# Splitting the first block's branch outputs into an attention half and a convolution half, and leaving 28 convolution taps until after the attention

## The chip, the cores and the metric

The kernel runs on one core of a Trainium2 chip. The metric is the device time of one execution in microseconds (us), the median of several runs. A difference of about 0.3% is what a measurement of this kernel can tell from no change.

The core has five engines that this document speaks of by the profile's names: PE (TensorE, matrix products; PEld is its weight load), DVE (VectorE), ACT (ScalarE), POOL (GpSimd) and SP (SyncE, which here issues the weight transfers). Each runs its own list of instructions in order; they wait for each other by semaphores. SBUF is the on-chip memory, PSUM the eight banks into which PE accumulates.

## The reference, cut to what matters

Two transformer blocks on 512 tokens of width 1024, all in float32. The change touches the first block alone, between its attention and the product with `w_out`:

```python
y_attn = nsa_attention(q, ...) @ w_attn_br[l]
y_conv = conformer_conv(u_conv, conv_dw_w[l], conv_dw_b[l], conv_ln_g[l], conv_ln_b[l], w_conv_br[l])
g_a, g_b = jnp.split(jax.nn.sigmoid(g_merge), 2, axis=-1)
x = x + (g_a * y_attn + g_b * y_conv) @ w_out[l]
```

```python
def conformer_conv(u, dw_w, dw_b, ln_g, ln_b, w_proj):
    a, gate = jnp.split(u, 2, axis=-1)
    z = a * jax.nn.sigmoid(gate)
    z = causal_dwconv(z, dw_w) + dw_b        # 31 taps, 512 channels
    z = jax.nn.silu(layer_norm(z, ln_g, ln_b))
    return z @ w_proj
```

## The kernel before, in words

**Layout and weights.** Activations lie transposed: channels on the 128 partitions, 512 tokens along the row. Every large product is cut into *units*. A unit is 128x1024 weights: eight blocks of 128x128, each used in three float32r matmuls of 512 columns (high part by high part, high by low, low by high), 24 matmuls in all. SP loads a unit's raw weights into one of five slots as soon as PE has finished with the unit five places earlier (`unit_done`); POOL then splits them into `whi` (L1055, L1056) and `wlo = raw - whi` (L1059); PE waits for `w_split`. So POOL's work comes once per unit, at the pace at which PE finishes units. The table `UNITS` gives the order of the units, here ... `ga` 0 to 7, `gb` 0 to 7, `y` 0 to 7, `wout` 0 to 7.

**Attention loop.** 32 steps (4 head pairs, 2 branches, 4 query tiles). In each, PE does scores (L568), transposes (L578), a quarter of a `ga` unit (six matmuls, L461) and values (L590). Scores go into two PSUM banks, one per half, and PE may write the next step's scores only when DVE has read these (`n_max`, L1847). DVE does `n_max` and, between, the *taps*: the convolution of the second branch is 4 chunks of channels times 31 taps = 124 instructions `cacc = z*w + cacc` (L1721), each on 128x512 elements, two of its inputs in SBUF. 46 of them are done before the loop. In the loop `taps(1)` is called in each of the first 12 steps and the other 66 are spread over the last 20 (4 or 3 a step). The attention to compressed keys adds more DVE work in the first ten steps (L1886 to L1906).

**After the attention.** PE does `gb` 1 to 7. Between them it takes column sums for the layer norm of the convolution: `mu` sums (four of them, one for each channel chunk, L515) after `gb` 1, a broadcast of the mean (`spread`, L549) after `gb` 2, variance sums after `gb` 3 and 4, their broadcast after `gb` 5. DVE centers (L1917), computes the reciprocal root, scales (L1928), and with ACT does SiLU (L1935 with ACT L1316 and L1321) and splits the result in high and low parts (ACT L1325, DVE `low_z` L1940). Then come eight `y` units. Unit `y` i makes output chunk i: half 0 is `w_attn_br` (four blocks, 12 matmuls, into bank 2 or 3), half 1 is `w_conv_br` (bank 6 or 7). DVE merges per chunk: L1982 multiplies the attention part by its gate, L1986 the convolution part, L1989 adds; ACT makes the high part (L1328), DVE the low part (L1975). The eight `wout` units take those as input; the first of them waits chunk by chunk.

## Time and profile before

| | us |
|---|---|
| median of 3 runs | 1352.49 |
| lowest, highest | 1349.76, 1352.93 |
| the profiled execution | 1354.35 |
| its span | 1351.9 |

| engine | busy us | share of the span |
|---|---|---|
| PE | 1313.4 | 97% |
| PEld | 1034.9 | 77% |
| DVE | 824.1 | 61% |
| POOL | 647.6 | 48% |
| ACT | 442.4 | 33% |

Durations below are from the profiled execution, which is 1.9 us above the median; its span is the time from the first to the last record, and 2.5 us lie around it. PE's busy time is modelled at its ends: matmuls overlap, so one that is listed with 0.39 us is followed by the next after 0.23 us. The pace is to be read from starts.

### The profile page before, as it was taken

The numbers are of one execution on the slowest core, as the hardware profiler recorded it, in microseconds if no ns is written. First come the engines' busy times: TensorE is split into PE (matmuls) and PEld (weight loads), VectorE is DVE, ScalarE is ACT, GpSimd is POOL, SyncE is SP. The second block draws the span as 40 slices with busy tenths as digits, with TensorE's granted clock in tenths as the row PEclk, the third lists the DMA queues.
The fourth block names the chain that finished last, engine by engine and source line by source line (L and its number), as shares of the span: only waits on it lengthen the run. The fifth ranks groups of instructions, "written<-read, shape, count | busy, mean of one in ns | idle before, by whom it ended". The sixth has DMA issues, their size and how long they took to land. (4 is left out here: it accounts for less than half of the span.)

```text
span 1351.9 us, 19692 instructions
## 1 busy us (share of the span) xinstructions
PE 1313.4 (97%) x7254; PEld 1034.9 (77%) x7254; DVE 824.1 (61%) x1586; ACT 442.4 (33%) x948; POOL 647.6 (48%) x523
## 2 busy tenths in 40 slices
PE   7999999999999999999999999999999999899996
PEld 5898776688888888888888888876657888666675
DVE  4898689914554777777773546536765552156643
ACT  4201555523121211222110432256665231244521
POOL 5775222246676666666676365532000566523230
PEclk9999999999999999999999989999999999899998
DMA  4622110112253455555552124211000223211011
GB/s 180 241 67 78 32 43 22 47 62 80 94 174 123 156 197 199 195 187 190 195 176 94 60 90 155 78 48 32 1 1 1 94 69 95 76 48 32 32 48 62
DMA packets 37522, 130.24 MB, mean 96 GB/s; under 512 B 4544, under 2 KB 4800, under 8 KB 37184
## 3 DMA queue, kind: packets, MB, share of 16 engines
q1 hardware_dynamic: 26640, 93.11, 21.2%
q10 hardware_dynamic: 10800, 35.98, 7.2%
q8 instruction: 58, 0.95, 0.3%
q14 instruction: 24, 0.20, 0.1%
HBM read 126.98 MB, written 2.10 MB: 95 GB/s over the span
## 5 line engine op out<-in xcount | busy, mean ns | idle before, releaser
L1059 POOL TENSOR_TENSOR wlo<-raw,whi 128x1024 fp32r<-128x1024 f32 x171 | 419.2, 2451 | 14.3
L1055 POOL TENSOR_TENSOR whi<-raw,ones 128x2 fp32r<-128x2 f32 x171 | 48.8, 285 | 654.2 <-DMA raw<-in_w 654.0
L461 PE MATMUL bank<-ysplit,whi 128*128 128x512 f32 x984 | 313.3, 397 | 0.9 <-POOL wlo L1059 0.9
L461 PE MATMUL bank<-hhi,whi 128*128 128x512 f32 x536 | 219.0, 409 | 0.8 <-DVE arena L2179 0.4
L461 PEld LDWEIGHTS bank<-ysplit,whi 128*128 128x128 f32 x984 | 183.6, 189 | 37.3 <-POOL wlo L1059 1.3
L461 PE MATMUL bank<-hhi,wlo 128*128 128x512 f32 x536 | 210.7, 393 | 0.0
L461 PE MATMUL bank<-hlo,whi 128*128 128x512 f32 x536 | 210.2, 392 | 0.0
L461 PE MATMUL bank<-ysplit,wlo 128*128 128x512 f32 x496 | 194.2, 392 | 0.0
L1056 POOL TENSOR_SCALAR whi<-raw 128x1022 fp32r<-128x1022 f32 x171 | 186.0, 1088 | 0.0
L461 PEld LDWEIGHTS bank<-hhi,whi 128*128 128x128 f32 x536 | 101.4, 189 | 26.3 <-issue 7.3
L461 PEld LDWEIGHTS bank<-hhi,wlo 128*128 128x128 f32 x536 | 101.4, 189 | 22.3
L461 PEld LDWEIGHTS bank<-hlo,whi 128*128 128x128 f32 x536 | 101.8, 190 | 18.3
L461 PEld LDWEIGHTS bank<-ysplit,wlo 128*128 128x128 f32 x496 | 93.7, 189 | 20.1
L1721 DVE SCALAR_TENSOR_TENSOR arena<-first,arena 128x512 f32<-128x512 f32 x120 | 103.5, 912 | 0.2
L1346 ACT ACTIVATE arena<-bank,cols 128x512 f32<-128x512 f32 x44 | 34.4, 781 | 177.7 <-DVE bank L2041 177.7
L2203 DVE CUSTOM_DVE_ANT_0 arena<-bank,arena 128x512 f32<-128x512 f32 x64 | 44.2, 690 | 44.6 <-PE bank L864 26.6
L760 PE MATMUL bank<-hhi,whi 128*128 128x512 f32 x176 | 68.5, 389 | 0.0
L760 PE MATMUL bank<-hlo,whi 128*128 128x512 f32 x176 | 68.5, 389 | 0.0
L760 PE MATMUL bank<-hhi,wlo 128*128 128x512 f32 x176 | 68.5, 389 | 0.0
L2041 DVE TENSOR_TENSOR bank<-bank,arena 128x512 f32<-128x512 f32 x44 | 30.7, 699 | 50.4 <-PE bank L461 50.4
L1460 ACT ACTIVATE arena<-arena,nmax,stat 128x512 f32<-128x512 f32 x64 | 51.6, 808 | 12.8 <-DVE nmax L2207 10.2
L2025 DVE CUSTOM_DVE_ANT_0 arena<-bank,arena 128x512 f32<-128x512 f32 x80 | 51.7, 683 | 0.0
(315 smaller groups left out, 2105.5 us busy)
## 6 DMA issues: line engine op xcount, KB each, us to landing
raw<-in_w SPq DMA_DIRECT2D x171, 512.0 KB, 3.6
arena<-in_ada ACTq DMA_DIRECT2D x48, 512.0 KB, 4.3
xbuf<-in_xT ACTq DMA_DIRECT2D x12, 256.0 KB, 5.6
xbuf<-in_w ACTq DMA_DIRECT2D x1, 2048.0 KB, 11.3
first<-in_w ACTq DMA_DIRECT2D x1, 2048.0 KB, 8.3
out_t<-xbuf SPq DMA_DIRECT2D x8, 256.0 KB, 2.1
xbuf<-in_xT SPq DMA_DIRECT2D x4, 256.0 KB, 6.4
first<-in_uq ACTq DMA_DIRECT2D x1, 768.0 KB, 7.1
```

The source lines that it names most:

```text
L461: m = mm(b[:, :], w[:, s, k * P:(k + 1) * P], x, start=(k == 0 and part == 0), stop=(k == DC - 1 and part == 2))
L760: m = mm(b[:, :], w[:, u % WS, n * P:(n + 1) * P], x, start=(i == 0 and part == 0), stop=(i == FC - 1 and part == 2))
L1055: g.tensor_tensor(whi[:, s, 0:2], raw[:, s, 0:2], ones[:, :], ALU.mult)
L1056: g.tensor_scalar(whi[:, s, 2:D], raw[:, s, 2:D], 1.0, 1.0, ALU.mult, ALU.mult)\
L1059: g.tensor_tensor(wlo[:, s, :], raw[:, s, :], whi[:, s, :].bitcast(F32), ALU.subtract)\
L1346: A(ua[:, i % 4, :], bank.of(("up", i))[:, :], ACT.Identity, scale=col("ffw", order_up(i) * 3 + 2), bias=col("ffb", order_up(i)))\
L1460: A(abp[:, s % 3, half, :], abp[:, s % 3, half, :], ACT.Exp, bias=nmax[:, x:x + 1], scale=ab_scale(p, half, qt), accum_out=rsum[:, x:x + 1 ...
L1721: V.scalar_tensor_tensor(cacc[:, c, :], z[:, c, k:k + T], w, cacc[:, c, :], ALU.mult, ALU.add)\
L2025: V.tensor_tensor_reduce(ada[:, j % 2, at], bank.tiles[CACT[half]][:, :], ada[:, j % 2, at], 1.0, 0.0, ALU.mult, ALU.add, acc[:, j // (3 * ...
L2041: V.tensor_tensor(b[:, :], b[:, :], spread2, ALU.mult).then_inc(*dve_did.up(("un", i)))
L2203: link(V.tensor_tensor_reduce(abp[:, s % 3, half, :], bank.of(("S", "AB", s, half))[:, :], zero, 1.0, -3.0e38, ALU.add, ALU.max, nmax[:, x ...
```

## The change

1. The eight `y` units become four `ya` units and four `yc` units. A `ya` unit holds the attention weights of two output chunks, a `yc` unit the convolution weights of two. The bytes, the units and the matmuls are the same; the order is all of the attention's first. A new function `y_unit` does one; each half goes into the next of four banks (2, 3, 6, 7) and signals for itself.
2. The layer norm's work on PE moves back: `mu` sums from behind `gb` 1 to behind `gb` 5, their broadcast to behind `gb` 6, variance sums behind `gb` 7 and `ya` 0, their broadcast behind `ya` 1. ACT's squares and SiLU parts move with them.
3. `TAPS_LIGHT` goes, `TAPS_NSA = 50` comes: 50 taps are spread evenly over the 32 steps (1 or 2 a step), and the remaining 28 are done in one run when DVE has left the attention loop.
4. DVE multiplies the attention part by its gate in eight instructions `y_attn(0)` to `y_attn(7)`, placed between the layer norm's parts; the last loop then has, for each chunk, the convolution part's product, the sum and the low part.

```diff
@@ -49,7 +49,7 @@
     + [("q", i) for i in range(4)]
     + [("ga", i) for i in range(DC)]
     + [("gb", i) for i in range(DC)]
-    + [("y", i) for i in range(DC)]
+    + [("ya", i) for i in range(4)] + [("yc", i) for i in range(4)]
...
@@ -85,7 +85,8 @@
 PREP_Q = {12: 0, 13: 1, 16: 2, 17: 3, 20: 4, 21: 5, 24: 6, 25: 7}
 AB_FILL = [("ega", 3), ("egb", 0), ("egb", 1), ("egb", 2), ("egb", 3)]
 EOUT_FIRST = {32: ((0, 0, 3),), 33: ((0, 3, 6),), 34: ((1, 0, 7), (0, 6, 7)), 35: ((2, 0, 7),)}
-TAPS_LIGHT = 12
+TAPS_NSA = 50
+Y_BANKS = (2, 3, 6, 7)
 CMP_S, CMP_TURN, CMP_O, N_HIGH = (1, 3, 5, 7), (5, 7, 9, 11), (13, 15, 16, 17), (18, 20, 28, 36)
...
-LIN, SC, TR, OB = (0, 1), (2, 3), (4, 5), (6, 7)
+LIN, SC, TR = (0, 1), (2, 3), (4, 5)
...
@@ -710,34 +711,42 @@
                 if i in CMP_O:
                     cmp_values(CMP_O.index(i))
 
+            def y_unit(name, j):
+
+                u, c0 = UNIT[(name, j)], 4 if name == "yc" else 0
+                pe.wait_ge(w_split.sem, u + 1)
+                for half in range(2):
+                    if j == 0 and half == 0:
+                        for c in range(4):
+                            pe.wait_ge(*dve_did.at(("y", c0 + c)))
+                    b = bank.take(pe, Y_BANKS, (name, 2 * j + half))
+                    for k in range(4):
+                        kk = 4 * half + k
+                        for part, (w, x) in enumerate(((whi, yhi(c0 + k)), (whi, ylo(c0 + k)), (wlo, yhi(c0 + k)))):
+                            m = mm(b[:, :], w[:, u % WS, kk * P:(kk + 1) * P], x,
+                                   start=(k == 0 and part == 0), stop=(k == 3 and part == 2))
+                    if half == 0:
+                        m.then_inc(*pe_did.up((name, 2 * j)))
+                m.then_inc(*unit_done.up(u))
+
             for i in range(1, DC):
                 unit("gb", i)
-                if i == 1:
+                if i == 5:
                     stats("mu", CC, src=cacc, ready=lambda c: dve_did.at(("conv", c)))
-                if i == 2:
+                if i == 6:
                     spread("mu", 2)
-                if i == 3:
+                if i == 7:
                     sums("var", 0, CC)
                     sums("var", 1, CC)
-                if i == 4:
+            for j in range(4):
+                y_unit("ya", j)
+                if j == 0:
                     sums("var", 2, CC)
                     sums("var", 3, CC)
-                if i == 5:
+                if j == 1:
                     spread("var", 4)
-            for i in range(DC):
-                u = UNIT[("y", i)]
-                pe.wait_ge(w_split.sem, u + 1)
-                for half, pool in ((0, SC), (1, OB)):
-                    if i == 0:
-                        for c in range(4):
-                            pe.wait_ge(*dve_did.at(("y", 4 * half + c)))
-                    b = bank.take(pe, pool, ("y", i, half))
-                    for k in range(4):
-                        kk = 4 * half + k
-                        for part, (w, x) in enumerate(((whi, yhi(kk)), (whi, ylo(kk)), (wlo, yhi(kk)))):
-                            m = mm(b[:, :], w[:, u % WS, kk * P:(kk + 1) * P], x,
-                                   start=(k == 0 and part == 0), stop=(k == 3 and part == 2))
-                m.then_inc(*unit_done.up(u))
+            for j in range(4):
+                y_unit("yc", j)
 
             for i in range(DC):
                 unit("wout", i, first=(lambda k: dve_did.at(("m", k))) if i == 0 else None)
@@ -1307,22 +1316,20 @@
 
             for i in range(DC):
                 gb_evac(i)
-                if i == 2 or i == 3:
-                    for c in (2 * i - 4, 2 * i - 3):
+                if i >= 6:
+                    for c in (2 * i - 12, 2 * i - 11):
                         square("var", c, cacc[:, c, :], dve_did.at(("zc", c)))
-                if i == 5:
-                    for c in range(CC):
-                        act.wait_ge(*dve_did.at(("zn", c)))
-                        A(cacc[:, c, :], cacc[:, c, :], ACT.Identity, scale=col("lng", c), bias=col("lnb", c))\
-                            .then_inc(*act_did.up(("zu", c)))
-                        if c >= 2:
-                            act.wait_ge(*dve_did.at(("zs", c - 2)))
-                        act.wait_ge(*act_did.at(("zu", c)))
-                        A(hs[:, c % 2, :], cacc[:, c, :], ACT.Tanh, scale=0.5).then_inc(*act_did.up(("zt", c)))
-                if i == 6:
-                    for c in range(CC):
-                        act.wait_ge(*dve_did.at(("zs", c)))
-                        A(yhi(4 + c), cacc[:, c, :], ACT.Copy, scale=0.5).then_inc(*act_did.up(("zhi", c)))
+            for c in range(CC):
+                act.wait_ge(*dve_did.at(("zn", c)))
+                A(cacc[:, c, :], cacc[:, c, :], ACT.Identity, scale=col("lng", c), bias=col("lnb", c))\
+                    .then_inc(*act_did.up(("zu", c)))
+                if c >= 2:
+                    act.wait_ge(*dve_did.at(("zs", c - 2)))
+                act.wait_ge(*act_did.at(("zu", c)))
+                A(hs[:, c % 2, :], cacc[:, c, :], ACT.Tanh, scale=0.5).then_inc(*act_did.up(("zt", c)))
+            for c in range(CC):
+                act.wait_ge(*dve_did.at(("zs", c)))
+                A(yhi(4 + c), cacc[:, c, :], ACT.Copy, scale=0.5).then_inc(*act_did.up(("zhi", c)))
             for i in range(DC):
                 act.wait_ge(*dve_did.at(("mg", i)))
                 A(hhi[:, i, :], merged[:, i, :], ACT.Copy, scale=0.5).then_inc(*act_did.up(("mhi", i)))
@@ -1958,17 +1965,38 @@
                 if i - 1 in N_HIGH:
                     o_low(N_HIGH.index(i - 1))
                 if i < n:
-                    taps(1 if i < TAPS_LIGHT else -(-len(steps) // (n - i)))
+                    taps((i + 1) * TAPS_NSA // n - i * TAPS_NSA // n)
+            taps(len(steps))
+
+            def y_attn(i):
+
+                if i % 2:
+                    dve.wait_ge(*unit_done.at(UNIT[("ya", i // 2)]))
+                else:
+                    dve.wait_ge(*pe_did.at(("ya", i)))
+                if i == 0:
+                    dve.wait_ge(*act_did.at(("ga", DC - 1)))
+                V.scalar_tensor_tensor(merged[:, i, :], merged[:, i, :], 1.0, bank.of(("ya", i))[:, :],
+                                       ALU.add, ALU.mult).then_inc(*dve_did.up(("ya", i)))
+                bank.freed(("ya", i), dve_did, ("ya", i))
+
             neg_mean()
             for c in range(CC):
                 center(c)
+            y_attn(0)
             var_rstd()
+            y_attn(1)
+            y_attn(2)
             for c in range(CC):
                 scale_z(c)
+            y_attn(3)
             for c in range(CC):
                 silu_z(c)
+            y_attn(4)
             for c in range(CC):
                 low_z(c)
+            for i in range(5, DC):
+                y_attn(i)
 
             def merged_low(i):
                 dve.wait_ge(*act_did.at(("mhi", i)))
@@ -1976,16 +2004,17 @@
                                        ALU.mult, ALU.subtract).then_inc(*dve_did.up(("m", i)))
 
             for i in range(DC):
-                dve.wait_ge(*unit_done.at(UNIT[("y", i)]))
-                if i == 0:
-                    dve.wait_ge(*act_did.at(("ga", DC - 1)))
-                link(V.scalar_tensor_tensor(merged[:, i, :], merged[:, i, :], 1.0, bank.of(("y", i, 0))[:, :],
+                if i % 2:
+                    dve.wait_ge(*unit_done.at(UNIT[("yc", i // 2)]))
+                else:
+                    dve.wait_ge(*pe_did.at(("yc", i)))
+                dve.wait_ge(*act_did.at(("gb", i)))
+                if i:
+                    dve.wait_ge(*dve_did.at(("mg", i - 1)))
+                link(V.scalar_tensor_tensor(ytmp, gbt[:, i, :], 1.0, bank.of(("yc", i))[:, :],
                                             ALU.add, ALU.mult))
-                bank.freed(("y", i, 0), dve_did, ("link", dve_did.n - 1))
-                dve.wait_ge(*act_did.at(("gb", i)))
-                link(V.scalar_tensor_tensor(ytmp, gbt[:, i, :], 1.0, bank.of(("y", i, 1))[:, :],
-                                            ALU.add, ALU.mult))
-                bank.freed(("y", i, 1), dve_did, ("link", dve_did.n - 1))
+                bank.freed(("yc", i), dve_did, ("link", dve_did.n - 1))
+                dve.wait_ge(*dve_did.at(("ya", i)))
                 V.tensor_tensor(merged[:, i, :], merged[:, i, :], ytmp, ALU.add)\
                     .then_inc(*dve_did.up(("mg", i)))
@@ -2403,7 +2432,8 @@
         "k": lambda i: col(w_in, (at[3], at[5], at[1], at[2])[i]),
         "ga": lambda i: col(w_in, at[9] + i * P),
         "gb": lambda i: col(w_in, at[9] + D + i * P),
-        "y": lambda i: np.concatenate([col(a["w_attn_br"][0][n_rows], i * P), col(a["w_conv_br"][0], i * P)]),
+        "ya": lambda i: np.concatenate([col(a["w_attn_br"][0][n_rows], j * P) for j in (2 * i, 2 * i + 1)]),
+        "yc": lambda i: np.concatenate([col(a["w_conv_br"][0], j * P) for j in (2 * i, 2 * i + 1)]),
         "wout": lambda i: col(a["w_out"][0], i * P),
         "up": lambda i: col(up, order_up(i) * P),
```

The order of the instructions, as the two programs have it. Names are tiles: `arena` holds among much else the convolution's sums `cacc`, `first` its input `z`, `xbuf` the merged branch outputs, `ysplit` the high and low parts that PE multiplies, `bank` a PSUM bank.

DVE at the end of the attention, before (L1865 to L1877 finish the last head pair, L1911 is the mean, L1917 the centering):

```order
307 L1865 TENSOR_TENSOR hs<-bank,arena 128x512
308 L1869 TENSOR_TENSOR first<-first,hs 128x512
309 L1873 TENSOR_TENSOR first<-first 128x512
310 L1877 TENSOR_TENSOR ysplit<-first,ysplit 128x512
311 L1911 TENSOR_SCALAR stat<-bank 128x4
312 L1917 TENSOR_TENSOR arena<-arena,bank 128x512 x4
313 L1599 TENSOR_SCALAR bank<-bank 128x4
```

and in the changed kernel (its line numbers are 7 higher here; L1728 is the tap, L1979 is `y_attn`):

```order
307 L1872 TENSOR_TENSOR hs<-bank,arena 128x512
308 L1876 TENSOR_TENSOR first<-first,hs 128x512
309 L1880 TENSOR_TENSOR first<-first 128x512
310 L1884 TENSOR_TENSOR ysplit<-first,ysplit 128x512
311 L1728 SCALAR_TENSOR_TENSOR arena<-first,arena 128x512 x28
312 L1918 TENSOR_SCALAR stat<-bank 128x4
313 L1924 TENSOR_TENSOR arena<-arena,bank 128x512 x4
314 L1979 SCALAR_TENSOR_TENSOR xbuf<-xbuf,bank 128x512
315 L1606 TENSOR_SCALAR bank<-bank 128x4
```

28 taps have come between the attention's last low part and the mean, and the first `y_attn` stands between the centering and the variance.

DVE from the scaling by the reciprocal root to the merge, before:

```order
325 L1928 TENSOR_TENSOR arena<-arena,bank 128x512 x4
326 L1935 SCALAR_TENSOR_TENSOR arena<-hs,arena 128x512 x4
327 L1940 SCALAR_TENSOR_TENSOR ysplit<-arena,ysplit 128x512 x4
328 L1982 SCALAR_TENSOR_TENSOR xbuf<-xbuf,bank 128x512
329 L1986 SCALAR_TENSOR_TENSOR arena<-arena,bank 128x512
330 L1989 TENSOR_TENSOR xbuf<-xbuf,arena 128x512
```

and in the changed kernel:

```order
327 L1979 SCALAR_TENSOR_TENSOR xbuf<-xbuf,bank 128x512 x2
328 L1935 TENSOR_TENSOR arena<-arena,bank 128x512 x4
329 L1979 SCALAR_TENSOR_TENSOR xbuf<-xbuf,bank 128x512
330 L1942 SCALAR_TENSOR_TENSOR arena<-hs,arena 128x512 x4
331 L1979 SCALAR_TENSOR_TENSOR xbuf<-xbuf,bank 128x512
332 L1947 SCALAR_TENSOR_TENSOR ysplit<-arena,ysplit 128x512 x4
333 L1979 SCALAR_TENSOR_TENSOR xbuf<-xbuf,bank 128x512 x3
334 L2014 SCALAR_TENSOR_TENSOR arena<-arena,bank 128x512
335 L2018 TENSOR_TENSOR xbuf<-xbuf,arena 128x512
```

The attention's products stand in two places within the layer norm's chain and three behind it; the merge of a chunk is one product shorter.

PE at the `mu` sums, with its waits, before (the rows around are the last block of `gb` 1 and the first of `gb` 2):

```order
948 L461 MATMUL bank<-hhi,wlo 128x512
949 L515 MATMUL bank<-ones,arena 128x1 [waits ptc,dve_did]
950 L515 MATMUL bank<-ones,arena 128x1 x3
951 L515 MATMUL bank<-ones,arena 128x1 [waits dve_did]
952 L515 MATMUL bank<-ones,arena 128x1 x3
```

and in the changed kernel (around are `gb` 5 and `gb` 6):

```order
1044 L462 MATMUL bank<-hhi,wlo 128x512
1045 L516 MATMUL bank<-ones,arena 128x1 [waits ptc,dve_did]
1046 L516 MATMUL bank<-ones,arena 128x1 x3
1047 L516 MATMUL bank<-ones,arena 128x1 [waits dve_did]
1048 L516 MATMUL bank<-ones,arena 128x1 x3
```

The sums stand 96 matmuls, four units, further back; the waits for DVE's last taps are the same.

## Rows read from the trace of the kernel before

**Rows 1.** The page: busy us (share of the span) and instructions

```profile
PE 1313.4 (97%) x7254; PEld 1034.9 (77%) x7254; DVE 824.1 (61%) x1586; ACT 442.4 (33%) x948; POOL 647.6 (48%) x523
```

**Rows 2.** Waits of PEld, 185 to 275 us: line, released by, us, times, longest

```profile
PEld bank L568 <- DVE nmax L1847: 5.9, 4, 2.3
PEld bank L568 <- DVE arena L1721: 0.8, 1, 0.8
```

**Rows 3.** PE timeline: start, us, engine line op, tiles, count [idle before, releaser]

```profile
260.01 0.79 PE L568 MATMUL bank<-split_r 64*128 64x384 f32 x6 [2.08 <-DVE nmax L1847]
```

**Rows 4.** DVE: source view of L1721 (ns min/median/max), then timeline of taps

```profile
L1721 DVE SCALAR_TENSOR_TENSOR arena<-first,arena x120: 734/742/2876, 56.5 to 268.6; 128x512 f32<-128x512 f32 x120
...
90.46 18.41 DVE L1721 SCALAR_TENSOR_TENSOR arena<-first,arena 128x512 f32<-128x512 f32 x24
...
223.07 4.20 DVE L1721 SCALAR_TENSOR_TENSOR arena<-first,arena 128x512 f32<-128x512 f32 x3
```

**Rows 5.** POOL timeline: the split after those taps, and the one at 223 us

```profile
109.57 0.20 POOL L1055 TENSOR_TENSOR whi<-raw,ones 128x2 fp32r<-128x2 f32 x1 [15.82 <-DMA raw<-in_w]
...
223.21 2.85 POOL L1059 TENSOR_TENSOR wlo<-raw,whi 128x1024 fp32r<-128x1024 f32 x1
```

**Rows 6.** Steps 2 and 3 of the attention: DVE's timeline, then PE's

```profile
144.22 0.55 DVE L1847 CUSTOM_DVE_ANT_0 arena<-bank,arena 128x384 f32<-128x384 f32 x1
...
144.92 0.98 PE L568 MATMUL bank<-split_r 64*128 64x512 f32 x6
```

**Rows 7.** PE timeline: first matmul of gb 1, and the mu sums behind it

```profile
278.86 0.39 PE L461 MATMUL bank<-hhi,whi 128*128 128x512 f32 x1
...
284.30 3.63 PE L515 MATMUL bank<-ones,arena 128*128 128x1 f32 x32
```

**Rows 8.** DVE timeline: the last instruction of the attention

```profile
280.96 0.69 DVE L1877 TENSOR_TENSOR ysplit<-first,ysplit 128x512 fp32r<-128x512 f32 x1 [0.70 <-ACT ysplit L1282]
```

**Rows 9.** POOL timeline behind the attention: the low splits

```profile
284.14 2.35 POOL L1059 TENSOR_TENSOR wlo<-raw,whi 128x1024 fp32r<-128x1024 f32 x1
...
289.56 2.38 POOL L1059 TENSOR_TENSOR wlo<-raw,whi 128x1024 fp32r<-128x1024 f32 x1
```

**Rows 10.** Windows (busy, granted clock, DMA) at two places, a wait of PE

```profile
288.00:290.00 2.00, 2.00 (x8) 1.60 (x8) 0.12 (x1) 0.00 (x0) 1.65 (x3) 0.78 0.00 0
290.00:292.00 2.00, 2.00 (x6) 1.52 (x6) 0.00 (x0) 0.00 (x0) 1.94 (x1) 0.50 0.00 0
292.00:294.00 2.00, 2.00 (x9) 1.64 (x8) 0.00 (x0) 0.00 (x0) 0.00 (x0) 0.86 0.00 0
...
1174.00:1176.00 2.00, 1.50 (x7) 1.25 (x8) 0.81 (x4) 0.00 (x0) 1.66 (x3) 0.50 0.00 0
1176.00:1178.00 2.00, 2.00 (x6) 1.57 (x5) 0.45 (x4) 1.09 (x4) 1.92 (x1) 0.50 0.00 0
...
PE bank L974 <- DVE arena L2179: 3.5, 1, 3.5
```

**Rows 11.** Timelines of PE (broadcast), DVE (scaling, SiLU, low parts) and POOL (split)

```profile
315.77 1.05 PE L549 MATMUL bank<-ident,stat 128*128 128x128 f32 x8
...
316.93 2.48 DVE L1928 TENSOR_TENSOR arena<-arena,bank 128x512 f32<-128x512 f32 x4 [4.13 <-PE bank L549]
...
321.97 3.07 DVE L1935 SCALAR_TENSOR_TENSOR arena<-hs,arena 128x512 f32<-128x512 f32 x2 [0.34 <-ACT hs L1321]
324.97 2.48 DVE L1940 SCALAR_TENSOR_TENSOR ysplit<-arena,ysplit 128x512 fp32r<-128x512 f32 x4
...
328.45 2.40 POOL L1059 TENSOR_TENSOR wlo<-raw,whi 128x1024 fp32r<-128x1024 f32 x1
```

**Rows 12.** The merge: source view (ns), PE's first wout matmul, DVE's last low parts

```profile
L1989 DVE TENSOR_TENSOR xbuf<-xbuf,arena x8: 1006/1136/1317, 334.7 to 372.7; 128x512 f32<-128x512 f32 x8
...
371.10 0.39 PE L461 MATMUL bank<-hhi,whi 128*128 128x512 f32 x1
...
373.67 1.47 DVE L1975 SCALAR_TENSOR_TENSOR hlo<-xbuf,hhi 128x512 fp32r<-128x512 f32 x2
```

## The prediction

> **What bounds the kernel now.** The page first: PE is busy for 97% of the span [rows 1], so only what lets PE wait, or slows its clock, can move the time. The reader should then ask, for the stretch that the change touches, what PE waits for. The waits of PEld between 185 and 275 us name DVE's score reading (L1847) four times, 5.9 us together, and DVE's taps (L1721) once with 0.8 us [rows 2]; PE's own timeline shows such a gap, the longest, of 2.08 us ahead of the scores (L568) [rows 3]. From 268 to 420 us, `gb`, `y` and the first `wout` units, the waits of PE list nothing: that stretch runs at PE's pace. Third, why DVE is late: a tap takes 0.742 us by itself, 2.876 at worst; three taps at 223.07 took 4.20 us [rows 4]. In the same moment POOL ran a low split (L1059, 223.21 to 226.06) [rows 5]. The long run of 24 taps took 18.41 us [rows 4] while POOL was nearly idle (its next work is at 109.57 after 15.82 us of waiting, [rows 5]); one split fell into it. So taps in a row cost (18.41 - 2.1)/24 = 0.68, say 0.67 us each, and each L1059 that meets them costs 2.876 - 0.742 = 2.1 us more.
>
> The Trainium skill, "SBUF — State Buffer", section "Who interferes with whom", says that a DVE instruction with two SBUF inputs and a GpSimd one that reads SBUF exclude each other for a whole instruction, and that the issue order decides who blocks. The trace agrees on the blocking. This rule speaks against the change: behind the attention the splits come more often.
>
> **The change, part by part.**
>
> *The attention loop.* Removed: 28 taps, 28 x 0.67 = 18.8 us of DVE in a stretch where it is the late engine. But PE gets back only its waits: 5.9 + 0.8 = 6.7 us [rows 2]; by PE's own gaps, whose ends are modelled, it would be some 5 us. I take 6.3 gone, since single splits can still hit a tap (one or two a step remain): -6.3, between -5.0 and -6.7.
>
> *The first twelve steps* had one tap each and now have 18 in all. In the steps where DVE also serves the compressed keys there was no room: `n_max` of step 2 ends at 144.22 + 0.55 = 144.77 and PE starts the next scores at 144.92 [rows 6]. An extra 0.67 there costs 0.5; the like at two later steps gives +0.9 in all (0 to 1.5).
>
> *The 28 taps behind the loop.* This decides the sum. Let t be 278.86, the start of `gb` 1 on PE [rows 7]. A unit takes PE 284.30 - 278.86 = 5.44 us. DVE leaves the loop with L1877, 280.96 + 0.69 = 281.65 = t + 2.8 [rows 8]. The whole stretch shifts with the attention, so the distances hold. PE now wants the `mu` sums after `gb` 5, at t + 27.2, and the last of four sums some 2.7 us later. The taps alone need 18.8 us: done at t + 21.6, well ahead. But PE now finishes a unit every 5.44 us and POOL splits one as often: L1059 starts at 284.14 = t + 5.3 and 289.56 = t + 10.7 [rows 9], and so on at t + 16.1, 21.6, 27.0 and 32.5. Five of these lie in the way: 18.8 + 5 x 2.1 = 29.3, so the taps end at t + 32.1. PE's sums would end at t + 27.2 + 3.5 = 30.7; now the last can start at 32.2 and ends at 33.1: +2.4. In the loop two of five splits cost the taps 0.8 more (the step before L1059, L1056, gets in their way as well); half of that gives +2.8, my value. Bounds: 0, if PE's delays are fewer than five; +5.9, if the taps reach past t + 32.5 and meet a sixth split.
>
> *The clock.* Now: after the 3.6 us of one-column sums [rows 7] the granted clock falls to 0.50, the lower of the two levels (1.2 GHz), (0.22 x 2 x 2 + 2 + 0.14 x 2 x 2) = 3.4 us in all between 288 and 294 [rows 10], of which half, 1.7 us, is lost. The sums are still four in a row behind a dense unit, so this stays. With PE waiting as well it is longer: after a wait of 3.5 us the clock was at 0.50 through 1174 to 1178 [rows 10] and somewhat beyond, which cost 2 to 2.5. So +0.8 (0 to +1.7).
>
> *From the variance's broadcast to the first `yc` unit.* In both kernels PE has two units of work in between, 10.9 us, but before, half 0 of `y` 0 gave 2.7 us more. DVE's chain from L1928 (316.93) to the last L1940 (324.97 + 2.48 = 327.45) includes one hit by a split at 321.97 [rows 11]. PE begins its units at 315.77 + 0.81, so it would want the result at 327.46: no slack left. `y_attn(3)` hides behind ACT's tanh, `y_attn(4)` (0.7 us) does not: +0.8. A split starts at 328.45 [rows 11], 0.3 us after the new end; if it comes before the last L1940, it is 2.1 more. Between 0 and +2.9.
>
> *The merge.* Per unit DVE now has two chunks of three instructions of about 0.69 us (two L1975 took 1.47 [rows 12]), 4.1 us. L1989 meets a split in one of them: it took 1.136 us in the middle, 1.006 at least [rows 12], 0.45 more than alone; now it would begin 0.7 earlier and wait 1.2. Makes 5.3 of 5.44 us: DVE just keeps pace. At the end, before, the low part of the last chunk was ready at 373.67 + 1.47 = 375.14, PE wanted it seven blocks after 371.10, at 375.86 [rows 12]. The chain behind the last unit is no longer than before: +0.2 (0 to +1.5).
>
> *At nothing:* weight bytes, units, matmuls, SP's and ACT's queues. The `y_attn` products read PSUM, and such instructions (L1982, L1986) show no lengthening beside a split; they sit in DVE's idle time. Banks rotate over four, each freed 5 us before it is wanted.
>
> Sum: -6.3 + 0.9 + 2.8 + 0.8 + 0.8 + 0.2 = -0.8. From 1354.35 that is 1353.55; from the median 1352.49, 1351.7 us. The gain of the attention is spent behind it.
>
> **The rivals.** A difference is told from no change from 0.3%, 4.1 us, on.
>
> *The taps hide after all.* If splits cost the run less than I think (as in the run of 24, which met one), PE finds the sums ready: -6.3 + 0.9 + 0 + 0 + 0.5 = -4.9: 1347.6 us. For it: 5.6 us of slack without splits. Against: the splits are tied to PE's units, and every one in rows that met taps cost 2 us.
>
> *The split catches the taps a sixth time: slower.* If the taps slip by 0.4 us past t + 32.1, the split at t + 32.5 holds the last of them, and the wait is 5.9 instead of 2.8; the longer wait takes the clock's +1.7, and the same lock at the last L1940 adds 2.1: -0.8 + 3.1 + 0.9 + 2.1 = +5.3: 1357.8 us. It decides from about 0.4 us of lateness, less than one slowed L1056; against it: PE's wait also holds back the splits that its units trigger, and both places must be hit.
>
> *POOL yields instead.* By the skill's rule ("SBUF — State Buffer", same section) taps that are issued first would make POOL wait, not DVE. Here that would mean taps of 0.67 us throughout and later splits, with four slots of reserve: as the first rival, 1347.6 us. The 4.20 us for three taps speaks against it; it has 0.03 of the chance that the first rival has below.
>
> **How the numbers follow.** The sum above (within 4 us either way) 0.56; the first rival and its kin, -4.1 or better, 0.21; the second, or a smaller gain in the attention with the same losses, +4.1 or worse, 0.23. The range: down to the first rival, with nothing left out but its bound, 1347.2; up to the second, 1357.8. Faster 0.21, same 0.56, slower 0.23.
>
> **What would show it.** In the profile after: no wait of PE for the score reading over 1 us between the twelfth step and the end of the attention; the run of 28 taps lasting 29 to 31 us with taps of 2.8 us in it; a wait of PE for the taps ahead of the `mu` sums of 2 to 3 us; a clock of 0.50 for 3.4 to 7 us behind them; a wait of under 1 us before the first `yc` matmul; none before `wout`. I am wrong if the run of taps ends within 25 us, or if PE still waits for DVE inside the attention.

## The result, and the profile after

The changed kernel takes 1375.98 us (median of 4 runs, 1375.8 to 1376.71), the kernel before 1352.71 us beside it (1349.76 to 1357.28). The ratio is 1.016, with a 95% interval from 1.013 to 1.019: the change costs 22 to 23 us (23.3 between the medians, 21.6 by the ratio), where 1351.7 us and no measurable difference had been forecast. The profiled execution took 1376.71 us with a span of 1374.0 us, 22.1 us above the 1351.9 us of the one before.

In the changed kernel the lines have moved: `unit` is L462 (was L461), the one-column sums L516 (L515), the scores L569 (L568), the branch outputs L726 (L738), the score reading L1854 (L1847), the tap L1728 (L1721), the scaling L1935 (L1928), SiLU L1942 (L1935), the low parts L1947 (L1940) and L2003 (L1975), the merge L2014 and L2018 (L1986 and L1989), `y_attn` L1979, and POOL's three passes for a weight unit L1064, L1065 and L1068 (L1055, L1056 and L1059). Below, "high pass" is L1065, which rounds the weights, and "low pass" is L1068, which subtracts the rounded from the raw ones. The two together are a split.

What PE waited for, 100 to 430 us (engine, line, released by: us in total, times, longest), the first four of six lines:

```profile
PE bank L516 <- DVE arena L1728: 9.5, 1, 9.5
PE bank L462 <- DVE hlo L2003: 3.9, 2, 3.7
PE bank L726 <- DVE ysplit L1947: 3.9, 1, 3.9
PE bank L569 <- DVE nmax L1854: 2.1, 4, 0.7
```

The last line answers to [rows 2, 3]: where PE had waited 5.0 us for the score reading, 2.1 are left, and of these 1.8 lie in the first twelve steps, where before there were none. The three above it are new: before, nothing was listed between 268 and 420 us. The first is the wait for the taps, as a row of PE's timeline (start, duration, tiles, count, idle before and releaser), and below it stand the run of taps and one of the six splits of POOL that fell into it:

```profile
313.08 6.99 PE L516 MATMUL bank<-ones,arena 128*128 128x1 f32 x32 [9.54 <-DVE arena L1728]
...
278.90 36.11 DVE L1728 SCALAR_TENSOR_TENSOR arena<-first,arena 128x512 f32<-128x512 f32 x28
...
285.91 1.56 POOL L1065 TENSOR_SCALAR whi<-raw 128x1022 fp32r<-128x1022 f32 x1
287.55 2.71 POOL L1068 TENSOR_TENSOR wlo<-raw,whi 128x1024 fp32r<-128x1024 f32 x1
```

The run took 36.11 us and not 29 to 31. The sums, 3.63 us in [rows 7], took 6.99, since they stand at the lower of the two clock levels. The windows of PE (stretch, length, PE busy, granted clock, DMA share, GB/s) show 0.50 through the wait, the sums and the first half of `gb` 6:

```profile
308.00:313.00 5.00, 0.00 (x0) 0.50 0.00 0
313.00:320.00 7.00, 6.92 (x33) 0.50 0.00 0
320.00:325.00 5.00, 5.00 (x13) 0.51 0.00 0
325.00:330.00 5.00, 5.00 (x27) 1.00 0.16 34
```

The other two new waits, on DVE's side. The low parts, 2.48 us in [rows 11], take 5.48 us, and the SiLU passes ahead of them 5.56. In the merge one instruction of every unit or so is held for 2 us. The last low parts end at 393.64 + 3.43 = 397.07; PE's last `yc` unit ended at 388.05, and PE did six blocks of the first `wout` unit before it had to wait for the seventh:

```profile
349.74 2.48 DVE L1935 TENSOR_TENSOR arena<-arena,bank 128x512 f32<-128x512 f32 x4 [2.74 <-PE bank L550]
...
352.74 5.56 DVE L1942 SCALAR_TENSOR_TENSOR arena<-hs,arena 128x512 f32<-128x512 f32 x4
358.82 5.48 DVE L1947 SCALAR_TENSOR_TENSOR ysplit<-arena,ysplit 128x512 fp32r<-128x512 f32 x4
...
378.10 2.52 DVE L2018 TENSOR_TENSOR xbuf<-xbuf,arena 128x512 f32<-128x512 f32 x1
382.75 2.88 DVE L2003 SCALAR_TENSOR_TENSOR hlo<-xbuf,hhi 128x512 fp32r<-128x512 f32 x1
388.94 2.88 DVE L2003 SCALAR_TENSOR_TENSOR hlo<-xbuf,hhi 128x512 fp32r<-128x512 f32 x1
393.64 3.43 DVE L2003 SCALAR_TENSOR_TENSOR hlo<-xbuf,hhi 128x512 fp32r<-128x512 f32 x2
...
396.52 0.78 PE L462 MATMUL bank<-hhi,whi 128*128 128x512 f32 x1 [3.69 <-DVE hlo L2003]
```

Behind each of these two waits the clock falls once more (PE's windows):

```profile
361.00:365.00 4.00, 0.46 (x2) 1.00 0.44 131
365.00:370.00 5.00, 5.00 (x17) 0.66 0.01 3
...
392.00:396.00 4.00, 0.83 (x3) 1.00 0.27 78
396.00:401.00 5.00, 4.48 (x13) 0.66 0.90 311
```

A window of 5 us with a mean of 0.66 holds (1 - 0.66) x 2 x 5 = 3.4 us at the half clock. So 1.7 us are lost, twice.

Put together, by the starts of the same matmuls in both timelines (the forecast in us beside it):

| stretch | forecast | measured |
|---|---|---|
| attention loop, first twelve steps | +0.9 | +2.3 |
| attention loop, the other steps | -6.3 | -5.0 |
| wait for the 28 taps | +2.8 | +9.7 |
| clock in and behind the `mu` sums | +0.8 | +4.1 |
| up to the first `yc` matmuls | +0.8 | +5.8 (3.9 wait, 1.7 clock) |
| merge, first `wout` units | +0.2 | +6.1 (3.9 wait, 1.7 clock) |
| all that follows | 0 | -1.0 |
| sum | -0.8 | +22.0 |

The first twelve steps end at 184.78 us before and at 187.12 after (first scores of the step behind them); `gb` 1 starts at 278.86 before [rows 7] and at 276.18 after. The -1.0 at the end is the clock once more: behind the wait that [rows 10] show at L974 (3.5 us in both kernels), PE worked 5.5 us at the half clock before and 3.4 us after.

### The profile page after: what moved, and what is told of

Same layout as the page of the kernel before. It is cut to its first block and busy times, and to the rows that moved or that the text cites. A ratio compares the mean times of both kernels' runs of the same rounds, so it can differ in the third digit from the quotient of the medians.

```text
span 1374.0 us, 19700 instructions
## 1 busy us (share of the span) xinstructions
PE 1321.3 (96%) x7254; PEld 1040.8 (76%) x7254; DVE 844.3 (61%) x1586; ACT 442.7 (32%) x948; POOL 652.7 (48%) x523
## 5 line engine op out<-in xcount | busy, mean ns | idle before, releaser
L1068 POOL TENSOR_TENSOR wlo<-raw,whi 128x1024 fp32r<-128x1024 f32 x171 | 421.8, 2466 | 14.3
L1064 POOL TENSOR_TENSOR whi<-raw,ones 128x2 fp32r<-128x2 f32 x171 | 47.0, 275 | 672.1 <-DMA raw<-in_w 672.0
L462 PE MATMUL bank<-ysplit,whi 128*128 128x512 f32 x984 | 313.3, 397 | 0.9 <-POOL wlo L1068 0.9
L462 PE MATMUL bank<-hhi,whi 128*128 128x512 f32 x536 | 219.8, 410 | 4.6 <-DVE hlo L2003 3.9
L462 PEld LDWEIGHTS bank<-ysplit,whi 128*128 128x128 f32 x984 | 183.6, 189 | 37.4 <-POOL wlo L1068 1.3
L462 PE MATMUL bank<-hhi,wlo 128*128 128x512 f32 x536 | 211.2, 394 | 0.0
L462 PE MATMUL bank<-hlo,whi 128*128 128x512 f32 x536 | 211.1, 394 | 0.0
L462 PE MATMUL bank<-ysplit,wlo 128*128 128x512 f32 x496 | 194.2, 392 | 0.0
L1065 POOL TENSOR_SCALAR whi<-raw 128x1022 fp32r<-128x1022 f32 x171 | 190.3, 1113 | 0.0
L462 PEld LDWEIGHTS bank<-hhi,whi 128*128 128x128 f32 x536 | 101.9, 190 | 31.3 <-issue 7.0
L462 PEld LDWEIGHTS bank<-hhi,wlo 128*128 128x128 f32 x536 | 101.9, 190 | 22.5
L462 PEld LDWEIGHTS bank<-hlo,whi 128*128 128x128 f32 x536 | 102.2, 191 | 18.4
L1728 DVE SCALAR_TENSOR_TENSOR arena<-first,arena 128x512 f32<-128x512 f32 x120 | 113.4, 994 | 0.2
L462 PEld LDWEIGHTS bank<-ysplit,wlo 128*128 128x128 f32 x496 | 93.7, 189 | 20.0
```

What stands on the lines that cost most here:

```text
L462: m = mm(b[:, :], w[:, s, k * P:(k + 1) * P], x, start=(k == 0 and part == 0), stop=(k == DC - 1 and part == 2))
L1064: g.tensor_tensor(whi[:, s, 0:2], raw[:, s, 0:2], ones[:, :], ALU.mult)
L1065: g.tensor_scalar(whi[:, s, 2:D], raw[:, s, 2:D], 1.0, 1.0, ALU.mult, ALU.mult)\
L1068: g.tensor_tensor(wlo[:, s, :], raw[:, s, :], whi[:, s, :].bitcast(F32), ALU.subtract)\
L1728: V.scalar_tensor_tensor(cacc[:, c, :], z[:, c, k:k + T], w, cacc[:, c, :], ALU.mult, ALU.add)\
```

## The experiments

The theory after the result: (1) every split holds the back-to-back taps twice, 0.8 us by the high pass and 2.1 by the low pass, and six of them fall into the run; (2) the new order of units has a price of its own, the two waits of 3.9 us and their two falls of the clock, also made by splits; (3) the rest is the clock. The rivals stand with each run. Where the expectations count 36 steps in the loop, or 24 behind the first twelve, it is 32 and 20. Every ratio is to the kernel before on the same chip, in the same series, and is not the quotient of the two medians: it differs from that by up to 0.2%; the median of before was 1355.13 us beside the first four kernels, 1352.88 beside the next four and 1355.76 beside the last four.

**The order alone.**

```diff
-TAPS_NSA = 50
+TAPS_LIGHT = 12
...
-                    taps((i + 1) * TAPS_NSA // n - i * TAPS_NSA // n)
+                    taps(1 if i < TAPS_LIGHT else -(-len(steps) // (n - i)))
```

> The order alone: the changed kernel, but with the taps spread over the attention loop as in the kernel before (one in each of the first 12 steps, the other 66 in the last 24), so that none is left behind it. The eight split units of the branch outputs and the later statistics stay. The theory (the run of taps costs the wait of 9.7 us before the sums and the half clock in and behind them, and the late branch units cost waits of their own): the loop ends where it did before, 2.7 us later than in the changed kernel, TensorE does not wait at the sums, they last 3.5 us and not 6.9, but the waits of 3.9 us at the first convolution unit and some 4 us at the first output unit (the merge on VectorE) stay. 1352.7 + 3.9 + 3.9 + about 1 for the clock = 1361.5 us, between 1359 and 1364. The rival: both waits are only the lateness of the taps handed on, and the order by itself is worth nothing: 1352.7 us, within 1.5.

Measured: 1365.27 us (1364.77 to 1367.92), ratio 1.0093 (1.006 to 1.0126). The waits of PE, 120 to 420 us:

```profile
PE bank L569 <- DVE nmax L1854: 5.0, 4, 2.1
PE bank L462 <- DVE hlo L2003: 3.9, 2, 3.7
PE bank L726 <- DVE ysplit L1947: 3.9, 1, 3.9
```

The wait for the taps is gone, the sums take 3.63 us as in [rows 7], and the waits in the attention are back. The other two waits stand to the tenth as in the changed kernel, and so does the half clock behind them: 0.66 in both windows of 5 us. So the order by itself costs 3.9 + 3.9 + 1.7 + 1.7 = 11.2 us, which the series bears out (12.6 us by the middle of the ratio, 10.1 between the medians). The time came out above the forecast's 1359 to 1364 us for two reasons: the two falls of the clock cost 3.4 us and had been put at 1, and the kernel before itself took 1355.13 us in this series, not the 1352.7 of the forecast.

**Splits out of the run of taps.** For six units POOL's two passes become fills with constants; the second kernel keeps the high pass. Both leave out weights of these units, so they do not compute the reference.

```diff
+            def fill(turn, s):
+
+                pool.wait_ge(landed[s].sem, turn * 16 + 16)
+                g.memset(whi[:, s, :].bitcast(F32), 0.01).then_inc(w_hi.sem, 1)
+                pool.wait_ge(w_hi.sem, turn * WS + (s + 1))
+                g.memset(wlo[:, s, :].bitcast(F32), 0.0001).then_inc(w_split.sem, 1)
...
+                    if 32 <= turn * WS + s < 38:
+                        fill(turn, s)
```

> The changed kernel with GpSimd's two wide passes of the units 32 to 37 (gb5 to gb7 and ya0 to ya2), whose splits fall into the run of the 28 taps, replaced by two fills with constants. The high and the low part of these six units are then constants and not the weights, so the output is not the reference's; every other instruction stays. The theory (each split costs the taps 2.93 us, six of them 17.6 us): the taps run for 28 x 0.66 = 18.5 us and not 36.1, end 6 us ahead of gb5's end, and TensorE does not wait for them: 9.7 us of wait and the 3.4 us of slow sums behind it go, some 3 of the further dips of the clock perhaps: 1376.0 - 13.1 = 1362.9 us, down to 1360. The rival: back-to-back taps are slow by their own chain (each waits for the last one's write, or for the arena's banks), and the splits only lie beside it: the run stays at 30 us or more and the time above 1370.

> As the run that fills both parts, but with the pass that makes the high part left whole for the units 32 to 37; the pass with two inputs from SBUF, which makes the low part, is replaced by a fill with a constant, so the low part of these six units is wrong. The theory (a tap beside the two-input pass is held 2.1 us, a tap beside the one-input pass 0.8 us): the run of taps lasts 18.5 + 6 x 0.8 = 23.3 us, and its end comes 1 us ahead of gb5's end: no wait at the sums, 1362.9 us as without any split, at most 1 more. The rival: the two passes together hold one tap after the other as one event, and the one-input pass alone, once it meets back-to-back taps, holds them as long: 6 x 2.1 or more, the run over 30 us, the time 1370 or more.

Measured: 1362.63 us, ratio 1.0052 (1.0027 to 1.0077), and 1363.23 us, ratio 1.0068 (1.0037 to 1.01). DVE's taps and one fill of the first kernel, then the taps and one high pass of the second:

```profile
280.87 18.64 DVE L1744 SCALAR_TENSOR_TENSOR arena<-first,arena 128x512 f32<-128x512 f32 x28
...
287.61 0.96 POOL L1074 MEMSET whi<- 128x1024 f32 x1 [3.29 <-DMA raw<-in_w]
```

```profile
278.84 21.82 DVE L1746 SCALAR_TENSOR_TENSOR arena<-first,arena 128x512 f32<-128x512 f32 x28
...
285.71 1.56 POOL L1075 TENSOR_SCALAR whi<-raw 128x1022 fp32r<-128x1022 f32 x1
```

28 taps take 18.64 us, 0.666 each: there is nothing slow in their own chain. Four high passes met the second run (the other two came after its end), and 21.82 - 18.64 = 3.2 us is 0.8 for each. What is left of the 36.11 us, 36.11 - 18.64 - 6 x 0.8 = 12.7, is 2.1 for each low pass; this price is a difference, since no run has low passes without high ones. That a fill, which only writes SBUF, does not hold a tap is also what the Trainium skill says ("SBUF — State Buffer", section "Who interferes with whom"); the 18.64 us beside eight fills agrees. Against the changed kernel the time falls by 13.4 and 12.8 us (14.6 and 12.4 by the ratios). That is the 9.7 us of waiting and the 3.4 us of the slow sums, and no more: the other two waits and their falls of the clock are as in the changed kernel.

**Half as many taps behind the loop.**

```diff
-TAPS_NSA = 50
+TAPS_NSA = 64
```

> The changed kernel with 64 taps in the 36 steps of the loop and 14 behind it (50 and 28 in the changed kernel). The theory: the run behind the loop meets three splits, 14 x 0.66 + 3 x 2.93 = 18.0 us, and ends 9 us ahead of gb5's end, so TensorE waits for nothing at the sums; half of the loop's gain of 2.7 us is given back; the waits at the first convolution unit and at the first output unit stay: 1376.0 - 13.1 + 1.4 = 1364.3 us, between 1361 and 1366. The rival: the loss goes by the number of taps moved and not by the point where they outlast the five units: half of 23.3 us is left, 1364.4 us too, but then with 3 us or more of wait at the sums, and with these sums at the half clock.

Measured: 1364.83 us (1360.53 to 1369.09), ratio 1.0068 (1.0031 to 1.0105), and no wait for the taps:

```profile
284.51 18.15 DVE L1728 SCALAR_TENSOR_TENSOR arena<-first,arena 128x512 f32<-128x512 f32 x14
```

18.15 us is 14 x 0.666 + 3 x 2.94. The taps cost a wait only if their end passes the end of `gb` 5. The times of both theories were the same, so only the profile tells them apart here. It also shows something that matters below: the 32 sums stand in a row from 309.01 to 312.5 us, PE is busy, and here the clock does not fall (PE's window of 40 us around them):

```profile
305.00:345.00 40.00, 40.00 (x218) 1.00 0.24 78
```

**The taps alone, the old order.**

```diff
-TAPS_LIGHT = 12
+TAPS_NSA = 50
...
-                    taps(1 if i < TAPS_LIGHT else -(-len(steps) // (n - i)))
+                    taps((i + 1) * TAPS_NSA // n - i * TAPS_NSA // n)
+            taps(len(steps))
```

> The other half of the change alone: the kernel before, with its order of units and statistics (the sums right behind gb1), but with 50 taps in the loop and 28 behind it. Theory (what holds the taps is GpSimd's splits, and these come only as TensorE frees weight slots): TensorE ends gb1 5.4 us after gb1's start and stands at the sums; so only the two splits already due fall into the run, which lasts 28 x 0.66 + 2 x 2.93 = 24.4 us and not 36.1. Taps begin 2.7 us behind gb1's start as in the changed kernel, the wait is 27.1 - 5.4 = 21.7 us, the sums go at the half clock (3.4 us more, and about 2 behind it), and the loop is 2.7 us shorter: 1352.7 - 2.7 + 21.7 + 5.4 = 1377 us, between 1374 and 1380. The rival (the run is 36 us long whatever TensorE does): 12 us more wait, 1389 us. The late units cost nothing here: no wait at the first branch output, none at the first output unit.

Measured: 1374.56 us (1369.04 to 1376.32), ratio 1.0182 (1.0148 to 1.0216). Timelines of DVE and PE:

```profile
279.07 24.37 DVE L1721 SCALAR_TENSOR_TENSOR arena<-first,arena 128x512 f32<-128x512 f32 x28
...
301.51 6.99 PE L515 MATMUL bank<-ones,arena 128*128 128x1 f32 x32 [19.56 <-DVE arena L1721]
```

The same 28 taps on the same engine last 24.37 us instead of 36.11, because TensorE stood still and freed no weight slot after the first two. So TensorE's progress sets how often the taps are held: the work that was to cover them is what stretches them. The wait is 2 us shorter than forecast, since the first sum needs only the first of the four channel chunks, which is done three taps before the end. Neither of the two waits of the new order is there. Order alone +0.9%, taps alone +1.8%, both +1.6%: the new order covers half of the wait (19.56 us become 9.5), but takes 11 us for it. (The intervals of the last two ratios overlap, so their order is not shown.)

**The order without splits.** The run of the order alone, with fills for the units 37 to 47, whose weights it so leaves out.

```diff
+            for turn in (7, 8, 9):
+                for s in range(WS):
+                    if 37 <= turn * WS + s < 48:
+                        fill(turn, s)
+                    else:
+                        split(turn, s)
```

> The run of the order alone (taps in the loop as before), with GpSimd's two wide passes of the units 37 to 47 (ya2, ya3, the four of yc and the first five output units) replaced by fills with constants; these eleven units' high and low weights are then constants, the output is not the reference's. Its question is what makes the two waits that the order alone showed, 3.9 us at the first convolution unit and 3.7 us at the first output unit. Theory (VectorE, hit by the splits): the last four passes ahead of the convolution units last 2.8 us and not 5.5, the four before them too (5.6), so the first wait is gone; the merge of a unit of two tiles costs 4.2 us of VectorE against 5.3 of TensorE, so it no longer falls behind, and the second wait falls to 2 or less: 7 us less than the order alone, 1358 us by its 1365.3. Rival (the distance in units is too short in itself, splits or not: the merge of the last two tiles and ScalarE's parts come behind the last unit anyway): both waits stay within 1 us of 3.9 and 3.7, 1365.

Measured: 1355.18 us (1350.38 to 1360.56), ratio 1.0018 (0.9991 to 1.0045). The list of waits names neither wait, and the low parts run at their own pace:

```profile
346.65 2.49 DVE L1963 SCALAR_TENSOR_TENSOR ysplit<-arena,ysplit 128x512 fp32r<-128x512 f32 x4
...
372.98 1.47 DVE L2019 SCALAR_TENSOR_TENSOR hlo<-xbuf,hhi 128x512 fp32r<-128x512 f32 x2
```

So the distance in units is enough if nothing holds DVE, and both waits are made by splits. By the ratios it gained 10 us over the order alone (7.8 by the medians, each less its own before), where 7 had been expected: PE's windows are whole from 350 to 385 us, so the two falls of the clock went with the waits.

**A third order.** The halves mixed, so that the attention's first two units cover the chain and the merge work stays spread, and the statistics two or three units earlier than in the change (ACT's and DVE's parts, not shown in the cut, move with them); then the same with ten taps behind the loop. The last line of the cut is that of the second kernel.

```diff
-    + [("ya", i) for i in range(4)] + [("yc", i) for i in range(4)]
+    + [("ya", 0), ("ya", 1), ("yc", 0), ("yc", 1), ("ya", 2), ("yc", 2), ("ya", 3), ("yc", 3)]
...
-                if i == 5:
+                if i == 3:
                     stats("mu", CC, src=cacc, ready=lambda c: dve_did.at(("conv", c)))
...
-                    taps((i + 1) * TAPS_NSA // n - i * TAPS_NSA // n)
+                    taps(3 if i in TAPS_EXTRA else 1 if i < TAPS_LIGHT else -(-(len(steps) - TAPS_BEHIND) // (n - i)))
```

> A third order of the branch outputs, with the taps in the loop as in the kernel before: ya0, ya1, yc0, yc1, ya2, yc2, ya3, yc3; the sums behind gb3, their spread behind gb4, all four square sums behind gb5, the second spread behind gb6. Theory: the chain from the second spread to the first convolution unit has gb7, ya0 and ya1 in front of it, 16.1 us, and needs 12.7 by the kernel before and 14 with one more split: no wait there. VectorE's merge work is spread as before, about 2 tiles with both parts in two units, so it ends 1 us or less behind the last unit's: no wait over 1 us at the first output unit. So the order costs nothing: the time of before on the same chip, ratio 1.000, within 0.003. Rival (splitting the units into halves costs by itself: more splits fall on the merge passes, since their number for a unit of TensorE's work is the same but a tile now waits for two units): 3 to 4 us of wait at the first output unit remain, ratio 1.003.

> The third order, and ten taps behind the loop; in the loop one in each of the first twelve steps but three in steps 6 and 10, and 52 in the last 24 steps (66 before). Theory: the run behind the loop is 10 x 0.66 + 2 x 2.93 = 12.5 us, from 2.7 to 15.2 us behind gb1's start, and the sums stand behind gb3, at 16.3: no wait, no half clock. The loop gains 14 / 28 of the 4.9 us that its last 20 steps gained, and loses nothing in its first 12: 2.5 us; ratio 0.998, between 0.995 and 1.001. Rival (the gain of the loop was not the taps' number but the phase of the splits against the steps): the loop is as long as before or longer, ratio 1.000 to 1.004; or a third split falls into the run and TensorE waits 1.8 us and drops its clock: 1.003.

Measured: 1353.68 us, ratio 1.0011 (0.9987 to 1.0034), and 1350.69 us, ratio 0.9998 (0.9976 to 1.0019). The mixed order with all taps in the loop costs nothing that can be measured; of its waits behind the attention one is left:

```profile
PE bank L463 <- DVE hlo L1996: 0.7, 1, 0.7
```

With ten taps behind, the run was

```profile
278.89 12.57 DVE L1725 SCALAR_TENSOR_TENSOR arena<-first,arena 128x512 f32<-128x512 f32 x10
```

12.57 = 10 x 0.666 + 2 x 2.95, and no wait. `gb` 1 starts at 276.2, 2.7 us before that of the kernel before, and nothing is lost in the first twelve steps (the next scores start at 184.66). The ratio, 0.9998, does not show this gain, though its interval does not exclude the 0.998 that was expected. What stands against the gain in the profile was looked at in a second series of the same kernel.

**The one-column sums halved.**

```diff
+            halves = {3: (None, mu_sums), 4: (mu_sums, None), 5: (None, var_sums), 6: (var_sums, None)}
             for i in range(1, DC):
+                inner, outer = halves.get(i, (None, None))
+                part = unit("gb", i, inline=False)
+                for k in range(DC):
+                    part(k)
+                    if k == 3 and inner:
+                        inner(2)
+                        inner(3)
+                if outer:
+                    outer(0)
+                    outer(1)
```

> The third order with ten taps behind the loop once more, beside its version with halved sums: ratio to before 0.9995, between 0.997 and 1.001, two stretches of 3.4 us at the half clock behind the two runs of 32 sums.

> The third order with ten taps behind the loop, and the one-column sums, 32 matmuls in a row so far, in two halves of 16 with four chunks of a gb unit between them (mu: two behind gb3, two in the middle of gb4; the squares': two behind gb5, two in the middle of gb6). Theory: TensorE's two stretches of 3.4 us at the half clock, each right behind a run of 32 such sums in the profile of the kernel with ten taps behind, come of these runs; halved, neither comes, as with the halves of the squares' sums in the kernel before: gb4 and gb6 last 5.3 us instead of 6.9, 3.2 us less than the unhalved, ratio to before 0.996 to 0.997. Rival: the clock's falls are not tied to these sums and come elsewhere: ratio as without the halves, 0.999. Second rival: a half clock comes behind each half: 2 us more, 1.000.

Measured: 1352.43 us, ratio 0.9981 (0.9954 to 1.0008), for the mixed order with ten taps behind; with halved sums 1350.87 us (1343.48 to 1354.85), ratio 0.9955 (0.9935 to 0.9974). PE's windows around and behind the sums, unhalved first:

```profile
292.00:296.00 4.00, 4.00 (x35) 0.99 0.47 133
296.00:300.00 4.00, 4.00 (x12) 0.59 0.01 2
...
308.00:313.00 5.00, 5.00 (x40) 1.00 0.32 105
313.00:317.00 4.00, 4.00 (x12) 0.58 0.00 0
```

```profile
295.00:299.00 4.00, 4.00 (x27) 1.00 0.36 112
299.00:303.00 4.00, 4.00 (x28) 1.00 0.07 24
...
311.00:315.00 4.00, 4.00 (x28) 1.00 0.40 131
315.00:319.00 4.00, 4.00 (x27) 1.00 0.00 0
```

PE was busy without a gap in all of these, and yet in these two profiles the clock fell to the half behind each run of 32 sums, and behind none of the runs of 16. The merged square sums had cost the mixed order a fall that the halves of the kernel before do not have. The kernel with halved sums is faster than the kernel before by 0.45%, and with the next one it is the only version whose interval stays below 1. The wait for a score operand in its attention (3.7 us at L570, once; 1.7 in the kernel before) is of this one profile, with a fall of the clock near it.

**One edit to the kernel before.** Only its 32 `mu` sums are halved (16 behind `gb` 1, eight each behind two chunks of `gb` 2); then also a table with three taps in each of the steps 6 and 10.

```diff
-                unit("gb", i)
+                part = unit("gb", i, inline=False)
+                for k in range(DC):
+                    part(k)
+                    if k in (1, 3) and i == 2:
+                        sums("mu", 2 + k // 2, CC, src=cacc, ready=lambda c: dve_did.at(("conv", c)))
                 if i == 1:
-                    stats("mu", CC, src=cacc, ready=lambda c: dve_did.at(("conv", c)))
+                    for c in (0, 1):
+                        sums("mu", c, CC, src=cacc, ready=lambda c: dve_did.at(("conv", c)))
...
-                    taps(1 if i < TAPS_LIGHT else -(-len(steps) // (n - i)))
+                    taps(3 if i in TAPS_EXTRA else 1 if i < TAPS_LIGHT else -(-len(steps) // (n - i)))
```

> The kernel before with one edit: the 32 one-column sums of mu behind gb1 are halved (16 behind gb1, eight each behind the second and the fourth chunk of gb2); all else, the taps too, stays. Theory: the kernel before falls to the half clock for 3.4 us behind these sums; halved they leave the clock alone, and gb2 lasts 5.4 us and not 7.1: 1.7 us less, ratio 0.9987. Rival: the clock falls anyway, behind the second half: ratio 1.000.

> As the kernel before with halved mu sums, and another table of taps: three in each of the steps 6 and 10, where VectorE idles over 2 us, and so 62 and not 66 in the last 24; none behind the loop. Theory: the loop's gain goes by the number of taps in its last steps: 4 of 28 of the 4.9 us, 0.7 us, on top of the 1.7: ratio 0.998. Rival: the two steps' idle time was spoken for, and the first twelve steps lose as much: ratio as with the halved sums alone, 0.9987 or more.

Measured: 1350.0 us (1347.96 to 1353.66), ratio 0.9967 (0.9947 to 0.9987); with the table 1353.28 us, ratio 0.999 (0.997 to 1.0009). In the first, the windows that fell to 0.78 and 0.50 in [rows 10] are whole:

```profile
286.00:289.00 3.00, 3.00 (x23) 1.00 0.49 131
289.00:292.00 3.00, 3.00 (x21) 1.00 0.11 44
292.00:296.00 4.00, 4.00 (x26) 1.00 0.02 4
```

1.7 us were expected of it, 0.13%; the middle of the ratio says 0.33%, its interval reaches to 0.13%. The profiles show where more can come from. In that of the kernel before, the longest fall of the clock with PE at work stands far behind the change, in the second of two runs of 16 one-column sums (L532) with six wide matmuls between them:

```profile
780.74 1.84 PE L532 MATMUL bank<-ones,arena 128*128 128x1 f32 x16
...
784.59 3.41 PE L532 MATMUL bank<-ones,sqt 128*128 128x1 f32 x16
...
784.00:786.00 2.00, 2.00 (x11) 0.52 0.00 0
...
792.00:794.00 2.00, 2.00 (x7) 0.50 0.44 178
794.00:796.00 2.00, 2.00 (x15) 0.92 0.00 0
```

From 784 to 796 us that is 10.2 us at the half clock, 5.1 us lost. In the profile of the halved `mu` sums the clock is 1.00 in this whole stretch, though its matmuls are the same. The fall is in 11 of the 14 profiles of this document; the taps alone in the old order and the mixed order with all taps in the loop lack it too. So one profile of each cannot tell whether the edit or chance took it away.

The table did not pay: `gb` 1 starts at 282.3 in its profile against 280.7, with one more fall of the clock (1.7 us) in its attention, so the loop itself is equal. 62 taps in the last 20 steps are no better than 66; the gain in the loop came with 52 and fewer.

## Why the prediction was wrong

It named the places and the mechanisms: splits hold the taps, TensorE waits at the `mu` sums, the clock falls behind the wait, the first `yc` unit finds no slack. It mis-sized every term of the stretch behind the attention, and all to the same side. Most share one cause: how often, and where, a split meets DVE.

- *The 28 taps behind the loop* (+2.8, measured +9.7). Two terms failed. The high pass was counted at 0.8 us in "two of five splits", as in the loop, where taps come three at a time and a pass can fall between them, and only half of that went into the value (+0.4); in back-to-back taps every pass meets one: 0.8 in each, by the run without low passes. And the count: five splits were taken to t + 32.1, the sixth at t + 32.5 was left to a rival. With 2.93 for each of six, the prediction's own sum gives 2.7 + 28 x 0.666 + 6 x 2.93 = 38.9 us behind the start of `gb` 1, and the trace has 278.90 + 36.11 - 276.18 = 38.8. At 2.93 us the fifth split alone takes the end to t + 36.0, past the sixth: the margin of 0.4 us was less than the error of one row.
- *The rival "a sixth split"* was the right one and was priced by its last split alone, 5.3 us in all. What bounded the range, 1357.8 us, took the merge and most of the clock as in the forecast.
- *The clock* (+0.8, measured +4.1 at the sums, and two more falls of 1.7). The prediction priced one fall, and put those behind later waits at nothing. After a wait the sums themselves, 3.63 us in [rows 7], run at the half clock, which no row of before showed for this line; and each later wait of 3.9 us drew a fall of its own. The price of a fall behind a wait was read short as well: the one of [rows 10] lasts to 1180 us, 5.5 us of PE's work at the half clock, which is 2.7 us lost and not 2 to 2.5.
- *The first `yc` unit* (+0.8, bound 2.9, measured 5.8). No slack was the right reading. The chain had two hits by splits. The one in the SiLU passes was there before too [rows 11]: from the start of the scaling to the end of SiLU it is 8.6 us after (352.74 + 5.56 - 349.74) and 8.1 before (321.97 + 3.07 - 316.93), with one `y_attn` more. The step that failed is the hit in the low parts: 5.48 instead of 2.48 us, 3.0 us, which the forecast left out and its bound had at 2.1. With the two `y_attn` it makes the wait of 3.9 us, and the fall of the clock behind it, 1.7 us, was in neither.
- *The merge* (+0.2, bound 1.5, measured 6.1). "DVE just keeps pace", 5.3 of 5.44 us, had no reserve, and counted 1.2 us for a split where the instructions, now back to back, lose 1.8 (378.10) to 2.5 (381.85 to 385.56). The run without splits shows 4.1 us of work for a unit and no wait. Before, a low pass ran while DVE did the two products that read PSUM, which were not lengthened (0.69 us each), and L1989 was held only by its last 0.3 to 0.6 us; the change moved the attention's product away and brought the instructions with two SBUF inputs under nearly the whole pass.
- *The attention* (-6.3 and +0.9, measured -5.0 and +2.3). The lower bound of the gain was right: PE's own gaps, not PEld's. The first twelve steps lost more than the one step that was worked out: 1.8 of the 2.3 us are waits for the score reading.
- *POOL yields instead* fell: with taps in a row the low pass lasts 2.71 instead of 2.38 us and the high pass 1.56 instead of 1.06, so POOL pays 0.3 to 0.5 and DVE 2.1 and 0.8.

What stays open: whether the one edit to the kernel before gains more than its 1.7 us, or its ratio (0.9967) owes the rest to falls of the clock that come and go; why one run of 32 sums drew no fall; and where the falls of the clock in the attention come from, which one profile has and another of the same loop has not.

## What to carry to other kernels

Work of DVE that reads two operands from SBUF and is put back to back beside GpSimd passes has to be priced with every pass that will fall into it, and their number follows from the engine that triggers them: if the cover (here five units of matmuls) also triggers the disturber, more cover means a longer run. Where a chain just keeps pace in the profile before, count the edit that takes its gaps away as a loss, with the whole price of a hit. And a margin smaller than the spread of one of its rows is no margin: then the rival is the forecast.
